# Five attentions whose two token tiles run one after the other, or step by step together

## What is computed

```python
def dsa_mixer(...):            # sparse; layers 0 and 1 of the first stack
    logits = einsum('bqhd,bqkd->bqhk', qj, kg) * HEAD_DIM ** -0.5
    p = softmax(where(valid, logits, -inf));  out = einsum('bqhk,bqkd->bqhd', p, vg)

def mla_attention(...):        # second stack, layer 1
    s = (einsum('bqhd,bkhd->bhqk', qn, k_nope) + einsum('bqhr,bkr->bhqk', qr, k_rope)) * scale
    p = softmax(where(causal, s, -inf));      out = einsum('bhqk,bkhd->bqhd', p, v)

def memory_cross_attention(...):   # second stack, both layers
    s = einsum('bshd,bmhd->bhsm', q, k) * XA_HEAD_DIM ** -0.5
    p = softmax(s);                out = einsum('bhsm,bmhd->bshd', p, v) @ wo
```

## Time and profile before

| | |
|---|---|
| median of 3 runs | 2813.42 us (2812.7 to 2815.88) |
| the profiled execution | 2820.07 us |
| its span, first to last instruction | 2817.7 us |
| TensorE busy | 2357.3 us, 84% |
| VectorE busy | 1868.7 us, 66% |
| ScalarE busy | 1333.8 us, 47% |
| mean granted TensorE clock | 0.898 of full speed |
| HBM traffic | 211 GB/s over the span |

### The profile page before, as it was taken

How to read it: one execution, slowest core, us unless ns; L and a number is a source line. 1 busy time by engine, 2 the same in 40 slices (tenths; PEclk the granted TensorE clock), 3 DMA queues, 4 the chain that set the end, 5 groups by cost and what they waited for, 6 DMA issues and landing times.

```text
span 2817.7 us, 30853 instructions
## 1 busy us (share of the span) xinstructions
PE 2357.3 (84%) x11193; PEld 1935.7 (69%) x11193; DVE 1868.7 (66%) x1975; ACT 1333.8 (47%) x1416; POOL 42.2 (1%) x102
## 2 busy tenths in 40 slices
PE   4836899855689999999999999966869987476998
PEld 4726687744567787777777777846758876465786
DVE  7776766776468787878888887855444443544553
ACT  3412433522247676766776676742334443232542
POOL 1000000000000000000000000000000000000000
PEclk9856999976689999999999999977979998688999
DMA  8730687530159899999999998953315552131453
GB/s 304 259 108 15 212 294 279 189 105 0 45 172 357 304 354 314 353 314 336 334 334 340 323 344 306 359 201 120 124 44 181 191 176 87 60 105 59 136 179 127
DMA packets 412832, 594.81 MB, mean 211 GB/s; under 512 B 20315, under 2 KB 326726, under 8 KB 412742
## 3 DMA queue, kind: packets, MB, share of 16 engines
q1 hardware_dynamic: 407040, 586.55, 60.4%
q10 hardware_dynamic: 5702, 7.04, 0.7%
HBM read 592.47 MB, written 1.05 MB: 211 GB/s over the span
## 4 chain that ended last, share of the span: by engine, by line
PE 72%; DVE 13%; ACT 5%; issue 3%; DMA 3%; POOL 1%; SPq 0%; ACTq 0%; DVEq 0%; POOLq 0%
PE bank L136 21%; PE bank L138 20%; PE bank L137 20%; DMA ring<-in_moe_w_up 2%; DVE ring_rounded L645 1%; PE bank L2330 1%; PE bank L1135 1%; PE bank L1113 1%; DVE ring_rounded L287 1%; ACT L L1187 1%; PE bank L2290 1%; PE bank L2311 1%; PE bank L1651 1%; PE bank L1124 1%; PE bank L461 1%
## 5 line engine op out<-in xcount | busy, mean ns | idle before, releaser
L136 PE MATMUL bank<-ring_rounded,hT_rounded 128*128 128x512 f32 (+3 forms) x944 | 376.9, 399 | 50.2 <-DVE ring_rounded L287 47.4
L136 PE MATMUL bank<-ring_rounded,z_rounded 128*128 128x512 f32 x896 | 365.9, 408 | 24.9 <-DVE AT_rounded L2501 11.4
L645 DVE TENSOR_TENSOR ring_rounded<-ring,zT_rounded 128x2048 fp32r<-128x2048 f32 x147 | 336.9, 2292 | 62.9 <-ACT zT_rounded L637 61.1
L136 PE MATMUL bank<-ring_rounded,L_rounded 128*128 128x512 f32 x712 | 290.5, 408 | 15.8 <-DVE score_rounded L778 10.5
L637 ACT ACTIVATE zT_rounded<-ring 128x2048 fp32r<-128x2048 f32 x147 | 281.6, 1916 | 31.6 <-DMA ring<-in_moe_w_up 16.6
L136 PEld LDWEIGHTS bank<-ring_rounded,hT_rounded 128*128 128x128 f32 x944 | 183.0, 194 | 88.3 <-issue 54.4
L136 PEld LDWEIGHTS bank<-ring_rounded,z_rounded 128*128 128x128 f32 x896 | 170.6, 190 | 67.6 <-issue 21.5
L645 DVE TENSOR_TENSOR ring_rounded<-ring,PT_rounded 128x2048 fp32r<-128x2048 f32 x74 | 169.4, 2289 | 39.9 <-ACT PT_rounded L637 39.5
L645 DVE TENSOR_TENSOR ring_rounded<-ring,mix_rounded 128x2048 fp32r<-128x2048 f32 x71 | 162.5, 2288 | 29.3 <-ACT mix_rounded L637 29.0
L136 PEld LDWEIGHTS bank<-ring_rounded,L_rounded 128*128 128x128 f32 x712 | 134.3, 189 | 56.2 <-DVE ring_rounded L645 19.4
L637 ACT ACTIVATE PT_rounded<-ring 128x2048 fp32r<-128x2048 f32 x74 | 141.7, 1915 | 37.9 <-DMA ring<-in_moe_w_up 36.4
(11 more groups left out here) (464 smaller groups left out, 5547.4 us busy)
## 6 DMA issues: line engine op xcount, KB each, us to landing
ring<-in_moe_w_gate SPq DMA_DIRECT2D x224, 512.0 KB, 5.3
ring<-in_moe_w_up SPq DMA_DIRECT2D x224, 512.0 KB, 6.8
ring<-in_moe_w_down SPq DMA_DIRECT2D x224, 512.0 KB, 7.8
ring<-in_ffn_w_gate_up SPq DMA_DIRECT2D x88, 512.0 KB, 5.1
ring<-in_ffn_w_down SPq DMA_DIRECT2D x66, 512.0 KB, 7.9
ring<-in_w_ada SPq DMA_DIRECT2D x48, 512.0 KB, 7.1
ring<-in_w_in SPq DMA_DIRECT2D x32, 512.0 KB, 4.9
xn<-in_w_ada SPq DMA_DIRECT2D x24, 512.0 KB, 9.6
```

Source lines behind the costliest of these rows:

```text
L136: pe.matmul(out, r32(a[0]), r32(b[1]), start=start, stop=False, skip_group_check=True)
L645: dve.tensor_tensor(r32(w), w, high(hi[slot]), ALU.subtract).then_inc(sem_out, 1)
```

## The change

Each attention gets, for each of its two tiles, a buffer `L`, a buffer `PT` and score banks of its own, and `nmx`, `esum`, `rsum` for each. In the sparse attention tile 0 uses the dead half rows of `xn`, in MLA those of `ada`. The transposes' banks are given by `turn`. TensorE multiplies the scores of both tiles before anything else, and then for each tile transposes and product. VectorE does the logits of tile 0, of tile 1, then the division of tile 0, of tile 1, then for each tile its copies and the subtraction. ScalarE takes the exponentials of both tiles and then does the copies of each. Tile 0 of the sparse and the MLA attention has its scores in two banks instead of four, so that two masked adds do what four did. The gate additions of layer 0, one or two at each of four places before, are now three (parts 3, 4, 5) between the divisions and tile 0's copies and two (6, 7) before tile 1's.

```diff
@@ -1102,16 +1102,24 @@
     return a
 
 
+def att_view(a, n):
+
+    s = a['keys'](n)
+    return a['L'][n].rearrange('p (h s) -> p h s', s=s)
+
+
 def attend_pe(c, pe, a):
     H = a['heads']
     for sem, v in a['ready']:
         pe.wait_ge(c.s[sem], v)
     for n in range(NT):
+        s = a['keys'](n)
+        for bank, rows in a['banks'][n]:
+            for u, i in enumerate(rows):
+                mm = pe.matmul(c.pb[bank][:, u * s:u * s + s], a['q'](i, n), a['k'](i, n), start=True, stop=True)
+        mm.then_inc(c.s['att_scores'], 1)
+    for n in range(NT):
         call, s = a['calls'][n], a['keys'](n)
-        for bank, rows in enumerate(a['banks']):
-            for u, i in enumerate(rows):
-                mm = pe.matmul(c.pb[bank][:, u * S:u * S + s], a['q'](i, n), a['k'](i, n), start=True, stop=True)
-        mm.then_inc(c.s['att_scores'], 1)
 
         pe.wait_ge(c.s['att_probs'], call['a'] + 1)
         nblk = att_blocks(a, n)
@@ -1121,8 +1129,8 @@
                 pe.wait_ge(c.s['att_PT_' + 'ab'[x % 2]], call['ab'[x % 2] + '0'] + x // 2 + 1)
             for blk in range(4 * b, min(4 * b + 4, nblk)):
                 ch, i = divmod(blk, H)
-                mm = pe.transpose(c.pb[4 + b % 3][:, (blk % 4) * P:(blk % 4) * P + P],
-                                  c.L[:, i * S + ch * P:i * S + ch * P + P], c.ident[:, :])
+                mm = pe.transpose(c.pb[a['turn'][b % 3]][:, (blk % 4) * P:(blk % 4) * P + P],
+                                  a['L'][n][:, i * s + ch * P:i * s + ch * P + P], c.ident[:, :])
             mm.then_inc(c.s['att_turned'], 1)
         pe.wait_ge(c.s['att_PT_a'], call['a0'] + (call['nb'] + 1) // 2)
         if call['nb'] > 1:
@@ -1132,65 +1140,80 @@
             pe.wait_ge(c.s['att_mixT'], call['a'])
         for out, terms in a['pv'](n):
             for x, (v, blk, m) in enumerate(terms):
-                mm = pe.matmul(out, v, c.PT[:, blk * P:(blk + m) * P], start=x == 0, stop=x == len(terms) - 1)
+                mm = pe.matmul(out, v, a['PT'][n][:, blk * P:(blk + m) * P], start=x == 0, stop=x == len(terms) - 1)
         mm.then_inc(c.s['att_out'], 1)
 
 
 def attend_dve(c, dve, a):
     H = a['heads']
-    L = c.L[:, :].rearrange('p (h s) -> p h s', s=S)
-    for n in range(NT):
+
+    def logits(n):
         call, s = a['calls'][n], a['keys'](n)
+        L = att_view(a, n)
         if a['mask'] is not None:
             for sem, v in a['mask_ready'](n):
                 dve.wait_ge(c.s[sem], v)
         dve.wait_ge(c.s['att_scores'], call['a'] + 1)
-        for bank, rows in enumerate(a['banks']):
+        for bank, rows in a['banks'][n]:
             m, i = len(rows), rows[0]
-            src = c.pb[bank][:, 0:m * S].rearrange('p (h s) -> p h s', s=S)[:, :, 0:s]
+            src = c.pb[bank][:, 0:m * s].rearrange('p (h s) -> p h s', s=s)
             if a['mask'] is None:
-                c.vstep(dve.tensor_copy(L[:, i:i + m, 0:s], src))
+                c.vstep(dve.tensor_copy(L[:, i:i + m, :], src))
             else:
                 mask = a['mask'](n).unsqueeze(1).broadcast_to([P, m, s])
-                c.vstep(dve.tensor_tensor(L[:, i:i + m, 0:s], src, mask, ALU.add))
-        c.vstep(dve.tensor_reduce(c.mx[:, 0:H], L[:, 0:H, 0:s], AX, ALU.max))
-        dve.tensor_scalar(c.nmx[:, 0:H], c.mx[:, 0:H], -a['scale'], None, ALU.mult)\
+                c.vstep(dve.tensor_tensor(L[:, i:i + m, :], src, mask, ALU.add))
+        c.vstep(dve.tensor_reduce(c.mx[:, 0:H], L, AX, ALU.max))
+        dve.tensor_scalar(c.nmx[:, n, 0:H], c.mx[:, 0:H], -a['scale'], None, ALU.mult)\
            .then_inc(c.s['att_max'], 1)
-        if 'fill' in a:
-            a['fill'](c, dve, n, 0)
+
+    def probabilities(n):
+        call, s = a['calls'][n], a['keys'](n)
+        L = att_view(a, n)
         dve.wait_ge(c.s['att_exp'], call['e0'] + H)
-        c.vstep(dve.reciprocal(c.rsum[:, 0:H], c.esum[:, 0:H]))
-        dve.tensor_tensor(L[:, 0:H, 0:s], L[:, 0:H, 0:s], c.rsum[:, 0:H].unsqueeze(2).broadcast_to([P, H, s]),
+        c.vstep(dve.reciprocal(c.rsum[:, n, 0:H], c.esum[:, n, 0:H]))
+        dve.tensor_tensor(L, L, c.rsum[:, n, 0:H].unsqueeze(2).broadcast_to([P, H, s]),
                           ALU.mult).then_inc(c.s['att_probs'], 1)
-        if 'fill' in a:
-            a['fill'](c, dve, n, 1)
-        nblk = att_blocks(a, n)
+
+    def take(n):
+        call, nblk = a['calls'][n], att_blocks(a, n)
         for b in range(1, call['nb'], 2):
             dve.wait_ge(c.s['att_turned'], call['t0'] + b + 1)
             w = min(4, nblk - 4 * b) * P
-            dve.tensor_copy(c.PT[:, 4 * b * P:4 * b * P + w], c.pb[4 + b % 3][:, 0:w]).then_inc(c.s['att_PT_b'], 1)
+            dve.tensor_copy(a['PT'][n][:, 4 * b * P:4 * b * P + w], c.pb[a['turn'][b % 3]][:, 0:w])\
+               .then_inc(c.s['att_PT_b'], 1)
 
         dve.wait_ge(c.s['att_mix_hi'], call['a'] + 1)
         lo, hi = a['out']
         dve.tensor_tensor(r32(c.hL[:, lo:hi, n * P:n * P + P]), c.pb[7][:, 0:(hi - lo) * P]
                           .rearrange('p (m t) -> p m t', t=P), high(c.hT[:, lo:hi, n * P:n * P + P]), ALU.subtract)\
            .then_inc(c.s['att_mixT'], 1)
+    for n in range(NT):
+        logits(n)
+    for n in range(NT):
+        probabilities(n)
+    for n in range(NT):
+        if 'fill' in a:
+            a['fill'](c, dve, n)
+        take(n)
 
 
 def attend_act(c, act, a):
     H = a['heads']
     for n in range(NT):
-        call, s = a['calls'][n], a['keys'](n)
+        call = a['calls'][n]
+        L = att_view(a, n)
         act.wait_ge(c.s['att_max'], call['a'] + 1)
         for i in range(H):
-            row = c.L[:, i * S:i * S + s]
-            act.activation(row, row, ACT.Exp, bias=c.nmx[:, i:i + 1], scale=a['scale'],
-                           accum_out=c.esum[:, i:i + 1]).then_inc(c.s['att_exp'], 1)
+            row = L[:, i, :]
+            act.activation(row, row, ACT.Exp, bias=c.nmx[:, n, i:i + 1], scale=a['scale'],
+                           accum_out=c.esum[:, n, i:i + 1]).then_inc(c.s['att_exp'], 1)
+    for n in range(NT):
+        call = a['calls'][n]
         nblk = att_blocks(a, n)
         for b in range(0, call['nb'], 2):
             act.wait_ge(c.s['att_turned'], call['t0'] + b + 1)
             w = min(4, nblk - 4 * b) * P
-            act.activation(c.PT[:, 4 * b * P:4 * b * P + w], c.pb[4 + b % 3][:, 0:w], ACT.Copy)\
+            act.activation(a['PT'][n][:, 4 * b * P:4 * b * P + w], c.pb[a['turn'][b % 3]][:, 0:w], ACT.Copy)\
                .then_inc(c.s['att_PT_a'], 1)
         act.wait_ge(c.s['att_out'], call['a'] + 1)
         lo, hi = a['out']
@@ -1221,7 +1244,10 @@
 def dsa_stage(core, k, evacuated):
     c = core
     order = [0, 2, 4, 1, 3, 5]
-    a = dict(heads=A_HEADS, scale=HD ** -0.5, banks=[[0, 1], [2], [3, 4], [5]],
+    first = c.xn[:, :, :].rearrange('p n d -> p (n d)')
+    a = dict(heads=A_HEADS, scale=HD ** -0.5, turn=(6, 0, 1), L=(first[:, 0:6 * P], c.L[:, 0:6 * S]),
+             PT=(first[:, D:D + 6 * P], c.PT[:, 0:12 * P]),
+             banks=(((0, (0, 1, 2)), (1, (3, 4, 5))), ((2, (0, 1)), (3, (2,)), (4, (3, 4)), (5, (5,)))),
              keys=lambda n: P * (n + 1),
              q=lambda i, n: c.rT[HD * (order[i] % 2):HD * (order[i] % 2) + HD, order[i] // 2, n * P:n * P + P],
              k=lambda i, n: c.rT[HD * (order[i] % 2):HD * (order[i] % 2) + HD, 3, 0:P * (n + 1)],
@@ -1235,8 +1261,8 @@
     if k == 0:
         st['own'] = [ada_job(core, 0, 2, i) for i in range(KD)]
 
-        def fill(c, dve, n, at):
-            dsa_gates(c, dve, st, ((3, 4), (5, 6, 7))[n][at:at + 1 + at * n])
+        def fill(c, dve, n):
+            dsa_gates(c, dve, st, ((3, 4, 5), (6, 7))[n])
         a['fill'] = fill
     return st
 
@@ -1834,7 +1860,9 @@
 
 def xa_stage(core, ready):
     c = core
-    a = dict(heads=XA_HEADS, scale=XA_D ** -0.5, banks=[[0, 1], [2, 3]], keys=lambda n: S,
+    a = dict(heads=XA_HEADS, scale=XA_D ** -0.5, turn=(4, 5, 6), keys=lambda n: S,
+             banks=tuple(((2 * n, (0, 1)), (2 * n + 1, (2, 3))) for n in range(NT)),
+             L=(c.L[:, 0:D], c.L[:, D:2 * D]), PT=(c.PT[:, 0:D], c.PT[:, D:2 * D]),
              q=lambda i, n: c.zT[:, i, n * P:n * P + P], k=lambda i, n: c.zT[:, 8 + i, :], mask=None,
              pv=lambda n: [(c.pb[7][:, h * P:h * P + P],
                             [(c.z[:, ch, h * P:h * P + P], ch * XA_HEADS + h, 1) for ch in range(NT)])
@@ -2057,7 +2085,10 @@
 
 def mla_stage(core, ready):
     c = core
-    a = dict(heads=MLA_HEADS, scale=QKW ** -0.5, banks=[[0, 1], [2, 3], [4, 5], [6, 7]],
+    a = dict(heads=MLA_HEADS, scale=QKW ** -0.5, turn=(6, 0, 1), L=(c.ada[:, 0:D], c.L[:, :]),
+             PT=(c.ada[:, D:2 * D], c.PT[:, :]),
+             banks=(((0, (0, 1, 2, 3)), (1, (4, 5, 6, 7))),
+                    ((2, (0, 1)), (3, (2, 3)), (4, (4, 5)), (5, (6, 7)))),
              keys=lambda n: P * (n + 1),
```

(3 more changed lines are left out.)

## The result

The changed kernel takes 2770.81 us in the median (2766.6 to 2771.99, 4 runs), the kernel before takes 2814.65 in the same comparison (2812.7 to 2816.89, 4 runs). The ratio is 0.9834 with the interval 0.9815 to 0.9853, that is 41 to 52 us gained. The profiled execution took 2771.99 with a span of 2770.3; before, 2820.07 and 2817.7.

What follows compares the result with a forecast made beforehand. The prediction took each attention as one chain of latencies, with no load waits behind. Terms of 39.9 us plus 3.7 for TensorE's clock, 43.6, off 2813.4 gave 2769.8 us, range 2762 to 2783.

Steps and rivals of the forecast that it cites:

- The bound: All five attentions: each is one chain of latencies, so a microsecond taken from an attention is a microsecond of the span.
- Which terms leave the path: Every attention: scores 1, exponentials 0, division 0 and transposes 0 less VectorE's copy for tile 0; 39.9 us in all.
- Layer 0: Sparse attention of layer 0: 8.0 us leaves, two gate additions lose their cover (4.7), 1.2 more goes; 2.0 gained.
- MLA: MLA attention: scores 1 6.2, exponentials 0 3.21, division and transposes 0 3.55, fewer adds 0.4; sum 13.4 us.
- Cross attentions: Two cross attentions: 7.7 and 8.5 us off the chains, plus 3.7 from product 1 halved by the clock in both.
- the bound of 5: Cross attentions: upper bound of the clock's gain, 5 us, with transposes 1 fast too; 3.7 was counted.
- Layer 1, the step that failed in size: Sparse attention of layer 1: scores 1 2.55, exponentials 0 2.45, division and transposes 0 2.85, fewer adds 0.4; sum 8.3 us.
- bounds 0 and 3: Sparse attentions: gain from a faster TensorE clock, between 0 and 3 us; nothing was counted.
- The narrow adds: Tile 0's masked adds, two for four: 0.4 us gained each in both sparse attentions and MLA; sparse bounds 0.4 and 0.8.
- Rival (4): All five chains: engines side by side slow each other; 43.6 us lost at a third longer, 2834 at half; chance 0.02.
- Rival (3): All attentions: tile 1's scores are held, tiles still run one behind the other; 2813, with fewer adds 2812; chance 0.03.
- Rival (1), the clock: Cross attentions: the clock does not rise for product 1; only 39.9 us gained, 2773.5 us; chance 0.25.

Runs made afterwards that it cites:

- the second experiment: Kernel before, with only the two cross attentions taking both tiles together, the sparse and MLA attentions unchanged: 2795.94 us, ratio 0.9927.
- the delays: Changed kernel with five more activations on ScalarE ahead of the exponentials of tile 0 (2770.07 us) or of tile 1 (2783.97 us), one run each.
- the early copy: Changed kernel with VectorE's copy of tile 0's transposes right behind division 0 instead of behind division 1: 2767.76 us in one run.
- only the scores first: Changed kernel with VectorE's and ScalarE's steps tile after tile again, only TensorE's scores of both tiles ahead: 2803.06 us, ratio 0.9955.
- early copy and spread additions: Changed kernel with tile 0's copy right behind division 0 and layer 0's gate additions spread one, two and two: 2756.6 us, ratio 0.9804.
- the longer exponentials 0: Changed kernel with five more activations of 128x256 on ScalarE ahead of tile 0's exponentials in each attention: 2770.07 us in one run.
- all three: Changed kernel with the early copy, the spread gate additions and idle matmuls in TensorE's waits together: 2749.0 us, ratio 0.9775.
- the longer exponentials 1: Changed kernel with five more activations of 128x256 on ScalarE ahead of tile 1's exponentials in each attention: 2783.97 us in one run.
- the filled waits: Changed kernel with idle matmuls in TensorE's waits ahead of transposes 0 and, in the cross attentions, behind product 1: 2762.55 us, ratio 0.9824.

## Why the prediction was right

The forecast was 2769.8 us, measured were 2770.81. The median is closer than the sum was: the five chains gained 47.45 in the two profiled executions, 3.9 more than the 43.6 of the sum. The interval of the ratio (41 to 52 us) holds both. The agreement within 1 us is in part luck, for two errors cancel. For the profiled execution the forecast had 2776.5, and 2771.99 was measured, 4.5 less. But it took 6.65 off for the median, as in the kernel before, and the median of the changed kernel is only 1.2 below its profiled execution. The terms of three stages came out by themselves, within 0.2 us in two and within 0.5 in the third; those of layer 1 and of the first cross attention were 2.2 and 0.9 too small.

- **The bound.** That a microsecond taken from an attention is one of the span held: 47.45 in the chains, 47.4 in the span, and in the second experiment, with two stages alone, 21.1 in the chains and 20.8 in the medians. TensorE's wait behind was the same 12.3.
- **Which terms leave the path.** Right, and tested from both sides by the delays: covered work in three stages cost next to nothing, uncovered work was paid everywhere. That VectorE's copy for tile 0 stays bare was right as well, and moving it is what the early copy gained (2.67 and 2.61 in layer 0 and MLA).
- **Layer 0.** 2.10 for 2.0 (the forecast's own terms, 8.0 less 4.7 less 1.2, give 2.1). The additions lost their cover as worked out. Spreading them brought 8.24 with the early copy and 2.67 came from the copy alone, so their place was worth 5.6.
- **MLA.** 13.53 for 13.4. Its scores were fast (32 records in 5.48), VectorE waited 0.58 for those of tile 1 (forecast 0.6), and product 1 began 24.66 behind the first scores (forecast 25).
- **Cross attentions.** To the start of product 1 it was 17.44 and 17.84, where the forecast had about 18.5 for the first. Product 1 took 2.02 at 1.00, forecast about 1.9. The term that was too small is the clock's: I halved product 1 alone, and the transposes 1 (1.04 and 1.53 for 1.97) and the end of product 0 (3.45 for 3.75, the first only) ran fast too. That lies within the bound of 5 which the forecast kept for it. The forecast's ground for the rise was thin, one place where the level had risen (2056.10). In the kernel before, MLA's product 0 and scores 1 ran at 0.50 for 8.1 us without a gap (2447.52 to 2455.60), so the rows before did not settle it; the experiments did, with 2.02 or 2.03 in both cross attentions of every paired kernel.
- **Layer 1, the step that failed in size.** 10.54 for 8.3. I took no clock here (bounds 0 and 3), since the trace of before had it at 0.50 throughout. Product 1 ran at 1.00, 1.3 us less. The other 0.9 is in scores 1: I had 1.5 us of them bare, from their time behind product 0 (3.95), but directly behind scores 0 the two together took 5.23 and VectorE waited 0.64. The granted clock of these scores was 0.50 before and after, so this is not the clock that I had counted for MLA's: joined to scores 0 without a stop, 2.24 and 3.95 became 5.23, which the forecast had at nothing.
- **The narrow adds.** The two of tile 0 took 1.15 in layer 1, as priced (0.56 each), and 1.42 in MLA, as priced (0.71 each).
- **Rival (4)** has no sign in the rows. Beside each other the exponentials took 0.49 to 0.51 and the copy 1.41 against 1.42 alone. (The forecast gave the new chains 22 to 31 us each, 128 in all; to the start of product 1 they took 17.4 to 45.2, 125.3 in all. The sum fits, the span of the five doesn't: layer 0's chain is the longest by far.) Rival (3) is excluded by the timeline.
- **Rival (1), the clock.** The Trainium skill (TensorE: Matmul & The Clock Gate, Why this matters for your kernels) warns of gaps between bursts. The forecast took from it that product 1 might stay slow, as gaps of 5 us remain ahead of the transposes 0. This case's trace agrees for what comes first behind such a gap, the transposes 0 and product 0 (1.97 and 3.45 to 3.75, the slow durations). Product 1 ran at 1.00 in spite of a wait of 1.18 us just before it, so the level came back within the attention: in the first cross attention it was 0.50 from 2040.17 to 2043.10 and 1.00 from 2043.20, still inside product 0. Where product 1 followed a wait of 7.8 us and the transposes 1, with only the scores first, it took 3.42.

What stays open: whether layer 1's product 1 runs in 1.52 or 2.83 differs from kernel to kernel. It was 1.52 in the changed kernel, with only the scores first, with the early copy and spread additions, with the longer exponentials 0 and with all three. It was 2.83 with the early copy alone, with the longer exponentials 1 and with the filled waits. The early copy stands in both groups (alone and with the spread additions, which change nothing in this stage's own order), and so do the filled waits. I have no cause for it, only the price of 1.3 us.

## What to carry to other kernels

Where a stage is one chain of latencies over engines and has two independent tiles, write the new chain down from the starts in the trace. What leaves is the first tile's steps up to where an in-order queue holds it back, and the sum was right to 0.2 us in two stages of five. Look then for the small copy that stands behind a long instruction of the other tile, and for filler whose cover has gone: moving both brought 13 us more by the chains. Count a step as gained only by what it leaves bare when it goes: 1.99 us of scores alone were worth 0.58.

## What the runs showed of the hardware that I had not expected

- The granted clock rises within one attention without any work being added: in both cross attentions of the changed kernel product 0 ran at or near the low level (3.45, 3.75) and product 1 at 1.00 (2.02). Product 1 took 2.02 or 2.03 in every experiment that pairs the tiles, and 3.42 and 3.63 in the one that doesn't.
- Idle matmuls can keep it up (transposes 0 1.09 for 1.97 in the cross attentions), but not in MLA, where 2.4 us of waiting lay behind them (1.97). After a further wait of 1.8 us product 0 was slow in one cross attention (3.60) and fast in the other (2.02).
- Two bursts of matmuls joined without a stop took less than the two apart at the same granted clock of 0.50: 5.23 us for 2.24 and 3.95 (scores of layer 1).
- The stretch of 1390 us between layer 1's attention and cross attention 1 took 1380.2 to 1392.8 us in the profiled executions, with the same instructions apart from the idle matmuls. A gain below some 5 us should be read from the stage, not from the time of one execution.
